# Two transformer blocks: a memory turn moved into the FFN's tail, x turned between keys and values, and a scale multiplied into the pooling weights

## The reference, cut to what matters

```python
mod = (silu(c) @ ada_w[i] + ada_b[i])            # 9 vectors of 1024: shift, scale, gate three times
x = x + 0.5 * (1 + gate0) * rmsnorm(swiglu(rmsnorm(x) * (1 + scale0) + shift0))
# the pooling mixer
h = rmsnorm(x) * (1 + scale1) + shift1
pooled = [centred_mean(h[group g], window 2, 4, 8, 16) for g in range(4)]
y = (einsum(pooled - h, pool_w) + pool_b) * pool_scale
x = x + (1 + gate1) * rmsnorm(y)
x = x + 0.5 * (1 + gate2) * rmsnorm(swiglu(rmsnorm(x) * (1 + scale2) + shift2))
...
kv = rmsnorm(mem) @ w_mem_kv                     # keys: 512 columns, values: 512 columns
```

## Time and profile before

| what | us |
|---|---|
| median of 3 runs (1780.09 to 1791.06) | 1782.03 |
| the profiled execution | 1781.23 |
| its span, first to last instruction | 1779.4 |
| TensorE busy (95% of the span) | 1682.2 |
| VectorE busy (68%) | 1206.7 |
| ScalarE busy (49%) | 866.8 |

### The profile page before, as it was taken

One profiled execution on the slowest core, in us unless ns is written; L12 is line 12 of the kernel. 1 busy time (PEld: TensorE's weight loads), 2 busy tenths in 40 slices (PEclk: granted clock), 3 DMA queues, 4 the chain that ended last, 5 costly groups with the idle time before them and its releaser, 6 DMA issues.

```text
span 1779.4 us, 20158 instructions
## 1 busy us (share of the span) xinstructions
PE 1682.2 (95%) x8007; PEld 1319.5 (74%) x8007; DVE 1206.7 (68%) x1703; ACT 866.8 (49%) x1237; POOL 48.3 (3%) x77
## 2 busy tenths in 40 slices
PE   6999998899999999989999999998989989999998
PEld 2788874578877888758778888776768887777876
DVE  2889765688856675543655555587477648988886
ACT  2545440434444444427544444554455337777775
POOL 1000000000000000000000001000000010000000
PEclk9999998999999999999999999999599989999999
DMA  9988645878849765440575544453023228989993
GB/s 353 376 300 291 233 138 206 296 259 297 285 152 317 238 191 191 168 160 5 170 231 188 179 161 121 154 166 118 19 77 107 95 57 304 358 311 327 331 330 142
DMA packets 201589, 373.80 MB, mean 210 GB/s; under 512 B 8880, under 2 KB 102486, under 8 KB 201488
## 3 DMA queue, kind: packets, MB, share of 16 engines
q1 hardware_dynamic: 188304, 324.67, 53.9%
q0 software_dynamic: 12784, 46.67, 7.6%
q10 hardware_dynamic: 400, 1.10, 0.2%
HBM read 371.36 MB, written 1.05 MB: 209 GB/s over the span
## 4 chain that ended last, share of the span: by engine, by line
PE 82%; DVE 10%; ACT 5%; DMA 2%; issue 1%; POOL 0%; SPq 0%; POOLq 0%; DVEq 0%; ACTq 0%
PE banks L519 22%; PE banks L521 22%; PE banks L520 22%; DVE ul L463 2%; PE banks L1231 2%; DMA raw<-in_ada_w 1%; PE banks L1258 1%; PE banks L741 1%; ACT uh L452 1%; PE banks L1708 1%; PE banks L861 1%; PE banks L2164 1%; ACT full L713 1%; PE banks L671 1%; PE banks L2209 1%
## 5 line engine op out<-in xcount | busy, mean ns | idle before, releaser
L463 DVE TENSOR_TENSOR ul<-raw,uh 128x1024 fp32r<-128x1024 f32 (+2 forms) x548 | 660.2, 1210 | 264.9 <-ACT uh L452 256.3
L452 ACT ACTIVATE uh<-raw 128x1024 fp32r<-128x1024 f32 (+2 forms) x548 | 572.1, 1050 | 484.1 <-PE banks L521 477.0
L519 PE MATMUL banks<-uh,hh 128*128 128x512 f32 (+2 forms) x1280 | 520.7, 407 | 15.2 <-DVE hl L778 7.2
L521 PE MATMUL banks<-uh,hl 128*128 128x512 f32 (+2 forms) x1280 | 498.6, 390 | 0.0
L520 PE MATMUL banks<-ul,hh 128*128 128x512 f32 (+2 forms) x1280 | 498.0, 389 | 0.0
L519 PEld LDWEIGHTS banks<-uh,hh 128*128 128x128 f32 x1280 | 242.7, 190 | 79.5 <-issue 12.5
L520 PEld LDWEIGHTS banks<-ul,hh 128*128 128x128 f32 x1280 | 242.8, 190 | 52.5 <-issue 7.4
L521 PEld LDWEIGHTS banks<-uh,hl 128*128 128x128 f32 x1280 | 242.4, 189 | 50.4
L519 PE MATMUL banks<-uh,bh 128*128 128x512 f32 x528 | 209.3, 396 | 10.7 <-DVE bl L910 5.7
L521 PE MATMUL banks<-uh,bl 128*128 128x512 f32 x528 | 205.9, 390 | 0.0
L520 PE MATMUL banks<-ul,bh 128*128 128x512 f32 x528 | 205.7, 390 | 0.0
(11 more groups left out here) (309 smaller groups left out, 1422.4 us busy)
## 6 DMA issues: line engine op xcount, KB each, us to landing
raw<-in_ffn_w_in SPq DMA_DIRECT2D x176, 512.0 KB, 5.1
raw<-in_w_up SPq DMA_DIRECT2D x64, 1024.0 KB, 5.7
raw<-in_ffn_w_out SPq DMA_DIRECT2D x44, 1024.0 KB, 6.5
arena<-in_ada_w POOLq DMA_DIRECT2D x38, 1024.0 KB, 7.6
raw<-in_ada_w SPq DMA_DIRECT2D x34, 1024.0 KB, 6.3
raw<-in_w_down SPq DMA_DIRECT2D x32, 1024.0 KB, 5.8
raw<-in_w_in SPq DMA_DIRECT2D x22, 1024.0 KB, 5.0
raw<-in_w_mem_kv SPq DMA_DIRECT2D x4, 1024.0 KB, 5.2
```

The costliest lines, as they stand in the source:

```text
L452: act.e.activation(uh[r][:, 0:w], raw[m % NRAW][:, h * w:(h + 1) * w], AF.Copy).then_inc(act_done, ta.put("hi", u))
L463: dve.e.tensor_tensor(ul[r][:, 0:w], raw[m % NRAW][:, h * w:(h + 1) * w], uh[r][:, 0:w].bitcast(F32), ALU.subtract).then_inc(dve_done, tv. ...
L519: pe.e.matmul(o, a, wh, start=s0, stop=False)
L521: mm = pe.e.matmul(o, b, wh, start=False, stop=s1)
```

## The change

It moves three things and changes two lists:

- Two more table pieces run within the first FFN (steps 9 and 10 of 11 get one each), two instead of four in the pool.
- The memory's turn, scaling and splitting are called as a `tail` of the first FFN, between its last spread and its last products. They now take the banks 4, 5, 7, 6 in this order; the last table piece of the FFN is ended ahead of them.
- x is turned for the pool between keys and values.
- `pool_scale` is multiplied by VectorE into the pool weights, in their slot, and into the bias, behind the first window. y then needs no scaling, and the pool's end uses `post_act` and `post_dve` as the FFNs do, which read the banks. The bias is added by four products of 512 columns ahead of the groups, in place of eight of 256.
- The pool weights stand ahead of the pool's table pieces in the list of chunks. GpSimd's loads for the next FFN wait for the pool's last product, in place of the scaling of y.

```diff
-ADA_AT.update({(0, 0, _b): _left.pop(0) for _b in range(8)})
-ADA_POOL = [_left.pop(0) for _ in range(4)]
+ADA_AT.update({(0, 0, _b): _left.pop(0) for _b in range(10)})
+ADA_POOL = [_left.pop(0) for _ in range(2)]
...
+    chunks.append((("pw",), [(I["pool_w"][0].rearrange("g (k p) n -> p (g k) n", p=P), 0)], 8, 256, False))
     for a in ADA_POOL:
         ada(*a)
-    chunks.append((("pw",), [(I["pool_w"][0].rearrange("g (k p) n -> p (g k) n", p=P), 0)], 8, 256, False))
     for a in ADA_GAP[0, 0]:
         ada(*a)
...
             spread(nb - 1)
+            if tail is not None:
+                tail()
             outp(nb - 1)
...
+        def mem_turn_pe(pe):
+            pe.later.flush()
+            turn_pe(pe, "mem", KD, lambda t, k: mrow[:, t, k * P:(k + 1) * P],
+                    lambda: pe.wait_ge(dve_done, tv("mem", 1)), bk=(4, 5, 7, 6), last=("tf",))
+
+        def mem_turn_act(act):
+            act.later.flush()
+            scaled_act(act, "mem", KD, hh)
+
+        def mem_turn_dve(dve):
+            dve.later.flush()
+            scaled_dve(dve, "mem", KD, hh, hl, lambda k: col("g_mem_2", k), lambda k: 0.0, bk=(4, 5, 7, 6))
+
         def kv_pe(pe):
-            turn_pe(pe, "mem", KD, lambda t, k: mrow[:, t, k * P:(k + 1) * P],
-                    lambda: pe.wait_ge(dve_done, tv("mem", 1)), last=("tf",))
             ready = parts_ready(pe, "mem")
             linear(pe, ("kv",), KD, lh, ll, ready, [[4], [5]], done=("k",))
+            turn_pe(pe, 1, KD, lambda t, k: x[:, t, k * P:(k + 1) * P], lambda: pe.wait_ge(dve_done, tv("dg", 1, 1)),
+                    bk=(0, 1, 2, 3), diag=True, last=("tf",))
             linear(pe, ("kv",), KD, lh, ll, ready, [[6], [7]], done=("v",))
...
         def pool_pe(pe):
-            turn_pe(pe, 1, KD, lambda t, k: x[:, t, k * P:(k + 1) * P], lambda: pe.wait_ge(dve_done, tv("dg", 1, 1)),
-                    bk=(0, 1, 2, 3), diag=True, last=("tf",))
+            m, w = take_raw(pe, ("pw",))
             for n, a in enumerate(ADA_POOL):
                 ada_parts_pe(pe, a, POOL_BANKS[n])
-            m, w = take_raw(pe, ("pw",))
-            pe.wait_ge(loaded("pool"), 48)
+            pe.wait_ge(dve_done, tv("pb"))
+            for b in range(4):
+                pe.take(b)
+                pe.e.matmul(PB[b], sum4[0:1, :], pbb[0:1, (b % 2) * 512:(b % 2) * 512 + 512], start=True, stop=False)
             for g in range(4):
-                if g == 2:
+                if g == 1:
                     for n, a in enumerate(ADA_POOL):
                         ada_total_pe(pe, a, POOL_BANKS[n], START_BUFS[n])
...
         def pool_act(act):
...
-            for t in range(T):
-                act.wait_ge(dve_done, tv("yp", t, 1))
-                squares_act(act, st[:, 4 + t:5 + t], xn[:, t, :], "sq", 1, t)
-            rstd_act(act, ("post", 1), T)
+            act.wait_ge(dve_done, tv("ada_e", ADA_POOL[-1]))
+            post_act(act, 1, "pool")
...
         def pool_dve(dve):
...
+                if g == 0:
+
+                    dve.wait_ge(ring[m % NRAW], landed[m])
+                    for gg in range(4):
+                        ww, pp = w[:, 2 * gg:2 * gg + 2, :], psb[:, gg * 256:gg * 256 + 256]
+                        dve.e.tensor_tensor(ww, ww, pp.unsqueeze(1).to_broadcast([P, 2, 256]), ALU.mult).then_inc(
+                            dve_done, tv.put())
+                    dve.e.tensor_tensor(pbb[0:1, :], pbb[0:1, :], psb[0:1, :], ALU.mult).then_inc(dve_done, tv.put("pb"))
+            for n, a in enumerate(ADA_POOL):
+                ada_end_dve(dve, a, POOL_BANKS[n])
             gap_skip(dve, ADA_GAP[0, 0])
-            dve.wait_ge(pe_done, tp("pool"))
-            for t in range(T):
-                for h in range(2):
-                    dve.e.tensor_tensor(xn[:, t, h * 512:(h + 1) * 512], PB[YB[t][h]], psb[:, h * 512:(h + 1) * 512],
-                                        ALU.mult).then_inc(dve_done, tv.put("yp", t, h))
-            for t in range(T):
-                dve.wait_ge(act_done, ta("sq", 1, t))
-                dve.own()
-                dve.e.tensor_tensor(xn[:, t, :], xn[:, t, :], G[1], ALU.mult).then_inc(dve_done, tv.put())
-            update_dve(dve, 1, 1.0)
+            post_dve(dve, 1, 1.0, "pool")
...
-            for n in range(1, 8):
+            for n in range(1, 10):
                 for c in range(2):
                     ada_load_pool(pool, n, c)
...
-            pool.wait_ge(dve_done, tv("yp", 1, 1))
+            pool.wait_ge(pe_done, tp("pool"))
             ada_loads_pool(pool, 0, 1)
```

More of the change, by code:

```diff
@@ L852, in y_frees, with ffn_pe @@
                     pe.frees(b, dve_done, tv, *name)
-        def ffn_pe(pe, q, nb, up, down, ready, between):
+        def ffn_pe(pe, q, nb, up, down, ready, between, tail=None):
             def spread(b):
@@ L881, in ffn_pe, with ffn_act @@
             spread(nb - 1)
+            if tail is not None:
+                tail()
             outp(nb - 1)
-        def ffn_act(act, q, nb, up, down, between):
+        def ffn_act(act, q, nb, up, down, between, tail=None):
             def spread(b):
@@ L903, in ffn_act, with ffn_dve @@
             spread(nb - 1)
+            if tail is not None:
+                tail()
             units_act(act, down(nb - 1), 2)
-        def ffn_dve(dve, q, nb, up, down, between, combine=False):
+        def ffn_dve(dve, q, nb, up, down, between, combine=False, tail=None):
             def spread(b):
@@ L939, in nothing, with sub_ffn_pe @@
             return None
-        def sub_ffn_pe(pe, i, s, gap=(), between=nothing):
+        def sub_ffn_pe(pe, i, s, gap=(), between=nothing, tail=None):
             q = i * 3 + 2 * s
@@ L951, in sub_ffn_pe, with sub_ffn_act @@
             pre_pe(pe, q, gap)
-            ffn_pe(pe, q, NFF, up_key(i, s), down_key(i, s), parts_ready(pe, q), side)
+            ffn_pe(pe, q, NFF, up_key(i, s), down_key(i, s), parts_ready(pe, q), side, tail)
             y_frees(pe, "x", q, 0)
             pe.later.flush()
-        def sub_ffn_act(act, i, s, gap=(), between=nothing, first=False):
+        def sub_ffn_act(act, i, s, gap=(), between=nothing, first=False, tail=None):
             q = i * 3 + 2 * s
@@ L965, in sub_ffn_act, with sub_ffn_dve @@
             pre_act(act, q, gap, first)
-            ffn_act(act, q, NFF, up_key(i, s), down_key(i, s), side)
+            ffn_act(act, q, NFF, up_key(i, s), down_key(i, s), side, tail)
             act.later.flush()
-        def sub_ffn_dve(dve, i, s, gap=(), between=nothing, first=False):
+        def sub_ffn_dve(dve, i, s, gap=(), between=nothing, first=False, tail=None):
             q = i * 3 + 2 * s
@@ L978, in sub_ffn_dve @@
             pre_dve(dve, q, gap, first)
-            ffn_dve(dve, q, NFF, up_key(i, s), down_key(i, s), side)
+            ffn_dve(dve, q, NFF, up_key(i, s), down_key(i, s), side, tail=tail)
             dve.later.flush()
@@ L1071, in kv_act @@
         def kv_act(act):
-            scaled_act(act, "mem", KD, hh)
             act.wait_ge(dve_done, tv("tl", "mem", 3))
@@ L2398, in tensor @@
             start_pe(pe)
-            sub_ffn_pe(pe, 0, 0, between=lambda b: pe.later.add(idle(*MEM_STEPS)) if b == 5 else None)
+            sub_ffn_pe(pe, 0, 0, tail=lambda: mem_turn_pe(pe),
+                       between=lambda b: pe.later.add(idle(*MEM_STEPS)) if b == 5 else None)
             kv_pe(pe)
@@ L2420, in scalar @@
             start_act(act)
-            sub_ffn_act(act, 0, 0, between=lambda b: act.later.add(mem_norm_act(act)) if b == 5 else None, first=True)
+            sub_ffn_act(act, 0, 0, tail=lambda: mem_turn_act(act),
+                        between=lambda b: act.later.add(mem_norm_act(act)) if b == 5 else None, first=True)
             kv_act(act)
@@ L2441, in vector @@
             start_dve(dve)
-            sub_ffn_dve(dve, 0, 0, between=lambda b: dve.later.add(mem_norm_dve(dve)) if b == 5 else None, first=True)
+            sub_ffn_dve(dve, 0, 0, tail=lambda: mem_turn_dve(dve),
+                        between=lambda b: dve.later.add(mem_norm_dve(dve)) if b == 5 else None, first=True)
             kv_dve(dve)
@@ L2480, in gpsimd @@
             gate_norm(2)
-            for n in range(1, 8):
+            for n in range(1, 10):
                 for c in range(2):
                     ada_load_pool(pool, n, c)
-            pool.wait_ge(dve_done, tv("ada_e", ADA_DVE[7]))
+            pool.wait_ge(dve_done, tv("ada_e", ADA_DVE[9]))
             load("pool", rc, I["rc_c"].rearrange("g n -> (g n)").unsqueeze(0).to_broadcast([P, 4 * S])
```

29 lines of the change are left out of this document (8 added, 21 removed).

## The result

| kernel | median, us | lowest to highest | runs |
|---|---|---|---|
| before | 1781.76 | 1780.09 to 1791.06 | 4 |
| changed | 1771.23 | 1770.23 to 1772.73 | 4 |

The ratio is 0.9927, with a 95% interval of 0.9904 to 0.995: 0.7% faster. The forecast was 1775 with a range of 1763 to 1789. The profiled execution took 1770.23 us, its span 1768.4 (before 1779.4). The same kernel, measured a second time beside two experiments, took 1774.14 us (1772.5 to 1774.96, 5 runs); the profiles of the two measurements differ by a spell of low clock in the pool, which the experiments take up.

A forecast was written before the change was run, and what follows sets the result against it. TensorE is busy nearly throughout, so only its waits and slow work yield time. Pool ends 20.8 us earlier (294.2), loads land at 313.3, turn 319.6 + 0.9 − 327.0 = −6.5: 1775 us, own range 1771 to 1780, with rivals 1763 to 1789.

The forecast's parts named there:

- wait for bank 7: In the tail, the memory's ninth turn waits until VectorE ends the last table piece at 240.0; about 1 us.
- wait for the diagonals: Between keys and values, TensorE waits 1.3 us for VectorE's diagonals before turning x.
- bias, pairs, totals: TensorE's pool products: four bias products 3.8 us, eight pairs of tile and group 9.0, two totals 1.9; together 14.7.
- The loads: Behind the pool, six chunks of Sync and GpSimd share one rate; the last lands 19.1 us after the pool's end.
- The pairs: In the pool, eight pairs of tile and group at 1.13 us each, 9.0 us.
- This part alone gains nothing: Keys, turn of x and values end at 273.8 against 273.7 before; it only buys time for VectorE.
- The scaling: VectorE's five operations scaling pool weights and bias take 4.0 us (3.5 to 6.1), costing nothing up to 7.9 us.
- the forecast without one: The forecast case, no low clock spell in the pool: 1775 us, own range 1771 to 1780, chance 0.55.
- the first rival: One low clock spell of 10.2 us in the pool costs 5.1 us: 1780 us, chance 0.17.
- the slower rival: Clock falls with the bias products and stays low until the pool's end: 28.0 instead of 14.7 us, 1788 to 1789, chance 0.11.
- The first quarter: First quarter of x's turn for the second FFN costs up to 0.9 us more at the low clock.
- The sum of −6.5: Turn for the second FFN at 319.6, plus 0.9 at the low clock, against 327.0 before: −6.5 us.

The follow-up runs named there:

- the runs with 128 rows: Bias products reading 128 rows instead of one; on the changed kernel 1774.06 us against 1771.23 and 1774.14, on the kernel with only the pool's part 1775.90 against 1783.06.
- The two parts: Against before: only the memory's turn in the tail and x turned between keys and values, 1777.88 us; only the pool's changes with the old turns, 1783.06 us.
- the pool alone: Against before: ten and two table pieces, pool weights ahead of the pieces, scale in the weights, both turns where they stood; 1783.06 us, ratio 0.9987 to 1.0016.

## Why the prediction was right, and where it was off

The changed kernel's first FFN began 0.98 us earlier than before's (first spread 65.22 against 66.20), which is within what the profiles of one kernel differ by there (65.22 and 66.54) and is not put down to the change. With 0.98 taken off the predicted times:

| step | predicted | measured |
|---|---|---|
| last spread ends | 236.2 | 236.07 |
| wait for bank 7 | 1 | 1.19 |
| post-norm starts | 248.0 | 248.36 |
| wait for the diagonals | 1.3 | 1.00 |
| keys, turn, values end | 272.8 | 272.32 |
| scaling | 4.0 | 3.6 |
| last window | 283.0 | 282.41 |
| bias, pairs, totals | 3.8, 9.0, 1.9 | 3.63, 7.10, 1.72 |
| pool ends | 293.2 | 290.42 |
| last gap chunk behind the pool | 19.1 | 18.92 |
| waits for the gap's chunks, together | some 15 | 12.2 |
| the last chunk's products, fillers | 6.3 | 5.96 |
| turn | 318.6 | 315.30 |

- **The loads** were the step that decided, and its size was right to 0.2 us. That it costs because GpSimd's packets share the rate with Sync's is shown by the hold of GpSimd's loads (10.8 us in place of 18.9). That it comes from the slot is shown by moving the weights' chunk alone, which brought back 15.6 us (24.9 to 9.3). The Trainium skill (DMA: Bandwidth & Descriptors, section "Issuing engines are not separate DMA queues") says, as the prediction has it, that loads run on the same 16 DMA engines and interleave, whichever engine started them. The runs agree: with GpSimd's queue held back, Sync's last chunk came 8.1 us sooner.
- **The pairs** were mis-sized: "eight pairs of tile and group at 1.13: 9.0". They took 7.10 (1.83 for two and 5.27 for six). The row of 1.13 stood between one-row products, and its duration reaches from the start of its first product to the end of its last, 0.07 us behind the next row's start (303.28 − 302.22 = 1.06). In runs of pairs a pair cost 0.88 to 0.92 from start to start.
- **"This part alone gains nothing"** of keys, turn and values was off: alone it moved the values' end by 2.6 us, and the kernel with it gained about 4 us. The prediction's list of waits before has 1.41 and 1.27 us but not the 1.33 ahead of the keys. In the change the bank wait and the second piece take most of the gain, so the sum there was off by only 0.5.
- **The scaling** lay in slack as said, and would still with 4.3 us more.
- **The clock.** In the first measurement's profile no spell came, and the forecast without one was the right case. But the first rival's mechanism is real. It came in the second measurement's profile, at 3.4 us where the rival priced 5.1 by a spell of 10.2. The chance of 0.17 was too low, and its argument against ("that spell came behind a wait") named the wrong condition: the wait is gone and the spell still came. Its argument for, the products with one single row, is what the runs with 128 rows bear out. No spell lasted to the pool's end, so the slower rival did not occur.
- **The first quarter.** The +0.9 us for the turn at the low clock was not paid. From the turn to the first spread it took 30.63 us, and 30.68 before.

The sum of −6.5 became −11.0 in the span. The step of 0.98 at the start, 3.3 up to the turn (2.8 of it there at the pool's end, of which 0.5 came with the earlier entry) and the 0.9 make 5.2; behind the second FFN's first spread 0.7 was lost again. Without the start-up's microsecond, and with a spell of 3.4, 6.6 of the 11.0 are left, about what was predicted for an execution without one: the errors of 4.2 up to the turn and in the quarter are about as large as a spell. So the mechanism was right, and the loads' size with it, but how near the total came is in part luck: these errors all fell on one side, and whether a spell comes in an execution decides as much. The second measurement, whose profile has the spell, shows 8.4 us (1782.57 to 1774.14).

The two parts are nearly additive in the stretch (3.2 + 3.9 = 7.1 alone, against 8.2 together in the profile with a spell and 11.6 in the one without) and not in the medians (4.4 gained and 0.8 lost, against 8.4 to 10.5 together). Since the pool alone loses time in runs that were not profiled, that difference is not settled.

## What to carry to other kernels

When a chunk is moved ahead in an in-order stream with a fixed number of slots, look at which chunk inherits its slot, and when its last reader gives it back: here the slot of the pool weights, given back by the pool's last product, fell to a chunk that was needed directly behind that product. Moving one chunk by two places was worth more (13 to 16 us in the medians) than the change itself (8 to 11). A transfer that is not urgent should wait for the urgent ones, whatever queue sends it. And a row's duration is a price only for instructions that stand as alone as that one did; for a run of them take the distance from start to start.

## What was not expected of the hardware

TensorE's granted clock fell from 1.00 (2.4 GHz) to 0.50 (1.2 GHz) for 3.4 to 6.8 us, 2.1 to 3.5 us behind the start of four products of one row by 512 columns, in six of seven profiles, and in four of these six TensorE had not waited once since the beginning of the values, some 20 us earlier. With 128 rows and the same number of products it stayed at 1.00 through the pool in five of five. Four products of 128 rows took 3.70 us and four of one row 3.69 at the same clock, so the filled rows cost no time.
